# Expert coefficient operands placed at byte remainders 160 and 448 by 512 in place of 320

## The reference, cut to what matters

```
qry    = x @ w_query                          # 8 heads, two halves of 128
s1, s2 = scores of the halves against 128 keys each
best, pos = the 16 best of the 256 sums of the 16 best of each
gate   = softmax(best)                        # 16 experts per head and token
hid    = gelu(x . u_tab[expert])              # 16384 experts, width 2048
y      = sum over experts of gate * hid * v_tab[expert]
out    = rmsnorm(h + y)
```

## Time and profile before

| | |
|---|---|
| median of 3 runs | 3287.17 us (3283.33 to 3290.22) |
| the profiled execution, its own time | 3283.08 us |
| its span, first to last instruction | 3281.0 us |
| PE busy | 3215.3 us, 98% |
| weight loads busy (beside PE) | 2870.7 us, 87% |
| DVE, ACT, POOL busy | 2041.9, 1459.9, 495.7 us |
| mean DMA rate | 196 GB/s |
| granted TensorE clock, mean | 0.994 of full |

### The profile page before, as it was taken

One profiled execution on the slowest core, in us unless ns is written; L12 is line 12 of the kernel. 1 busy time (PEld: TensorE's weight loads), 2 busy tenths in 40 slices (PEclk: granted clock), 3 DMA queues, 4 the chain that ended last, 5 costly groups with the idle time before them and its releaser, 6 DMA issues.

```text
span 3281.0 us, 48331 instructions
## 1 busy us (share of the span) xinstructions
PE 3215.3 (98%) x20054; PEld 2870.7 (87%) x20054; DVE 2041.9 (62%) x1849; ACT 1459.9 (44%) x1268; POOL 495.7 (15%) x418
## 2 busy tenths in 40 slices
PE   7999999999999999999999999999999999999998
PEld 6788899999999878878879999999999888888886
DVE  4455665555555656765456788999984555555554
ACT  5554454433343463463335434555543433333333
POOL 0000000000000002225400000888850000000000
PEclk9999999999999999999999999999999999999999
DMA  6444465555555443342236566676776666566563
GB/s 257 143 165 158 163 221 193 192 192 191 192 192 191 154 167 120 124 157 100 83 136 231 187 219 219 225 243 239 257 250 238 250 256 234 226 243 254 226 247 117
DMA packets 131396, 644.18 MB, mean 196 GB/s; under 512 B 14640, under 2 KB 47664, under 8 KB 61872
## 3 DMA queue, kind: packets, MB, share of 16 engines
q1 hardware_dynamic: 96016, 624.18, 53.0%
q10 hardware_dynamic: 35232, 17.83, 1.8%
HBM read 606.31 MB, written 35.66 MB: 196 GB/s over the span
## 4 chain that ended last, share of the span: by engine, by line
PE 92%; DVE 3%; ACT 2%; DMA 1%; issue 1%; SPq 1%; DVEq 0%; ACTq 0%
PE pj L290 12%; PE pj L292 12%; PE pj L291 11%; PE pj L278 7%; PE pj L277 7%; PE pj L276 7%; PE pj L1640 3%; PE pj L1642 3%; PE pj L1641 3%; PE pj L821 3%; PE pj L823 3%; PE pj L822 3%; PE pm L278 2%; PE pt L278 2%; PE pt L277 2%; PE pm L277 2%
## 5 line engine op out<-in xcount | busy, mean ns | idle before, releaser
L258 ACT ACTIVATE hi<-raw 128x2048 fp32r<-128x2048 f32 x535 | 1025.2, 1917 | 1381.3 <-PE pj L292 640.7
L265 DVE TENSOR_TENSOR lo<-raw,hi 128x2048 fp32r<-128x2048 f32 x400 | 918.5, 2296 | 678.3 <-ACT hi L258 677.5
L290 PE MATMUL pj<-xh,hi 128*128 128x256 f32 x3328 | 919.9, 276 | 0.0
L291 PE MATMUL pj<-xl,hi 128*128 128x256 f32 x3328 | 918.8, 276 | 0.0
L292 PE MATMUL pj<-xh,lo 128*128 128x256 f32 x3328 | 918.8, 276 | 0.0
L291 PEld LDWEIGHTS pj<-xl,hi 128*128 128x128 f32 x3328 | 625.0, 188 | 0.6
L290 PEld LDWEIGHTS pj<-xh,hi 128*128 128x128 f32 x3328 | 624.8, 188 | 0.6
L292 PEld LDWEIGHTS pj<-xh,lo 128*128 128x128 f32 x3328 | 624.8, 188 | 0.0
L265 DVE TENSOR_TENSOR lo_in<-raw,hi 128x2048 fp32r<-128x2048 f32 x135 | 311.4, 2309 | 277.6 <-ACT hi L258 276.9
L2317 POOL TENSOR_SCALAR hotA<-cst,slotT 128x128 fp32r<-128x128 f32 x256 | 337.3, 1333 | 473.1 <-ACT slotT L2160 435.8
L1640 PE MATMUL pj<-hi,xh 128*128 128x512 f32 x576 | 235.7, 409 | 13.4 <-ACT proj L1709 7.3
(11 more groups left out here) (382 smaller groups left out, 4253.2 us busy)
## 6 DMA issues: line engine op xcount, KB each, us to landing
raw<-w_peer SPq DMA_DIRECT2D x256, 1024.0 KB, 6.4
raw<-w_mlp SPq DMA_DIRECT2D x128, 1024.0 KB, 4.8
raw<-w_in SPq DMA_DIRECT2D x104, 1024.0 KB, 4.8
raw<-w_out SPq DMA_DIRECT2D x32, 1024.0 KB, 4.8
raw<-w_q SPq DMA_DIRECT2D x16, 1024.0 KB, 4.9
act_scratch<-hidU SPq DMA_DIRECT2D x32, 512.0 KB, 3.3
gates_scratch<-stage ACTq DMA_DIRECT2D x8, 2048.0 KB, 17.1
hidV<-act_scratch SPq DMA_DIRECT2D x32, 512.0 KB, 3.5
```

Source lines behind the costliest of these rows:

```text
L258: nc.scalar.activation(hi[:, j, :], raw[:, j, :], ACT.Copy).then_inc(hi_ready, 1)
L265: nc.vector.tensor_tensor(low(q)[:, j, :], raw[:, j, :], hi[:, j, :].bitcast(F32), ALU.subtract).then_inc(lo_ready, 1)
L290: nc.tensor.matmul(o, hi[:, j, cols], xh[:, k0 + k, :], start=clears, stop=False, skip_group_check=True)
L291: nc.tensor.matmul(o, hi[:, j, cols], xl[:, k0 + k, :], start=False, stop=False, skip_group_check=True)
```

## The change

It gives each of the four coefficient operand tiles of the down stage a remainder. With `at_raw` at remainder 128, buffer 0 (even superblocks) is put at (128 + 32) mod 512 = 160 and buffer 1 (odd superblocks) at (128 + 320) mod 512 = 448.

```diff
         coefV = y("coefV", [P, 4, TT * P])
-        cV_h = [y(f"cV_h{i}", [P, 4, TT * P], F32R) for i in range(2)]
-        cV_l = [y(f"cV_l{i}", [P, 4, TT * P], F32R) for i in range(2)]
+        cV_h = [y(f"cV_h{i}", [P, 4, TT * P], F32R, rest=(at_raw + (32, 320)[i]) % 512) for i in range(2)]
+        cV_l = [y(f"cV_l{i}", [P, 4, TT * P], F32R, rest=(at_raw + (32, 320)[i]) % 512) for i in range(2)]
         last_sq = y("last_sq", [P, TT, D])
```

## The result

The changed kernel is slower: 3302.61 us (3298.41 to 3304.39, 5 runs) against 3287.17 us (3283.33 to 3290.22). The ratio is 1.0043, with a 95% interval of 1.0032 to 1.0054: small, but clear of noise. The time lies inside the range that was given (3266 to 3303), at its upper end, but the direction is not the one that was forecast. The profiled execution took 3298.41 us with a span of 3296.6, 15.6 us more than before.

What follows compares the result with a forecast made beforehand. PE's matmul stream alone was taken to bound the kernel. All terms were 0, so the profiled execution would stay at 3283.08 us; with the runs' median 4.1 above that, the forecast was 3287 us, range 3266 to 3303.

Steps and rivals of the forecast that it cites:

- step 1: Down stage, ACT's and DVE's writes of `cV_h` and `cV_l`: even if doubled, covered by slack; taken as 0.
- step 3: Down stage, weight loads: 188 ns beside a matmul step of 228.9, 41 ns free, so covered; taken as 0.
- the slower pattern: Same addresses, triples (three matmuls) of 700 against 686.7 ns: +6.8 us for even superblocks alone, +13.6 for both buffers.
- The rival with 0.25: Here the one forecasting a slower down stage: stream locks into the slower of two patterns, 3294 to 3304 us; chance 0.25.
- number 4: Down stage, matmul step: claimed not to depend on the distance between stationary and moving operand; 0 for both buffers.
- The slower rival: Down stage: matmul stream locks into the slower of two patterns, 13.3 ns a triple, 3294 to 3304 us; chance 0.25.
- The faster rival: Down stage: step's surplus over 215 ns is a conflict of PE's two reads, set by distance; 3244 to 3280 us; chance 0.25.
- the 13 ns of "waste": Down stage: each matmul step's excess over the skill formula's 215.8 ns for 512 columns, 40 us in the stage as estimate.

## Why the prediction was wrong

*What held.* PE's step alone decides this stage; nothing of the 13.6 us came by ACT, DVE, DMA or the clock. The writes (step 1) and the length of the weight load (step 3) kept their times, and both were covered. I had given the price of the slower pattern as 13.3 ns a triple, +13.6 us for both buffers; the stage grew by 13.6 us, and buffer 0 alone cost its half, 6.9 us of stage (buffer 1 alone 10.2, of which some 3 are the seven neighbours it drew along, 0.42 us each). The rival with 0.25 was the outcome. That the time fell inside the range is that rival's doing, as its price was the upper end; my own forecast was no change.

*The step that failed is number 4*, "I take 0 for the odd buffer" and "I take the value of the nearest rows, 0" for the even one. The step went from 228.9 to 233.3 ns in both, 13.6 us in place of 0. It rested on three rows, and each was too far away:

- L1452 shows no difference between distances 0 and 192, in 128-column plain fp32 products. The 512-column fp32r stream does differ there, 680 against 686.7 ns a triple. By 256, moreover, these two distances are its only fast places of eight: the rows compared the two that cost least.
- L1030 and L1031 at distance 0 are four matmuls behind an interruption. I read their 233 ns as "within 5 ns", when 4.4 ns was the whole effect in question.
- The up stage at -192 runs at 113.3 ns, and from that I drew that the odd buffer would be no slower. With the roles exchanged and twice the columns the map is another: -192, which is 64 by 256, is fast in the up stage and slow in the down stage.

The slower rival had the right price with a wrong condition, and the price was in part luck. It was taken from a pattern in which every triple takes 700 ns. In the changed kernel the triples go to and fro between about 698 and 702 ns and only their mean is 700, so it is the same pace but not the same pattern. The rival laid the cost on a start that is no multiple of 64 and on the phase at entry. Remainder 448, a multiple of 64, cost as much as 160, and the remainders 0, 192 and 256 as much or nearly so. The phase at entry does choose between two patterns at distance 192, but at the other six no superblock had a mean step below 232.2 ns, and at distance 0 none above 227.1. The faster rival was wrong for this change, yet a small part of what it hoped for exists at a distance that the change didn't take: 2.2 ns a matmul at distance 0. Its floor of 215 ns came from L635, which is no like row: 256 columns of plain float32 take 215 ns there, and 256 fp32r columns 113.5 in the up stage. No 512-column fp32r step below 226.7 ns was seen to hold.

The Trainium skill, page "TensorE: Matmul & The Clock Gate", section "Part 2: What happens when you issue a matmul", says that loading the next weights takes no read bandwidth from the running matmul. The load's duration keeps its median of 187 or 188 ns in the down stages of all kernels, in agreement; but the time from matmul to matmul depends on the two operands' distance, from 226.7 to 234.2 ns in the down stages and from 113.5 to 120.1 in the up stages, so in this kernel the two are not without effect on each other. The trace doesn't show the reads themselves. The formula that the prediction weighed, from the same page's section "Back-to-back issue gap", is given there for an isolated matmul, not for a stream with a load for each, so the 13 ns of "waste" don't follow from it.

*What stays open.* Why the period is 256 bytes, and what in PE or in its reads makes the patterns, no run tells. Distances that aren't multiples of 32 weren't tried. In the up stages only three distances were seen. Why one way of mixing two fast places (22.18 us) is slower than either is open too, and so is what in a passing stage sets the pattern of the next.

## What to carry to other kernels

When PE is busy all of the time, the relative placement of the stationary and the moving operand, here modulo 256 bytes, is worth a few tenths of a per cent to 2%, and is found only by trying: put a different remainder into each of two alternating buffers, and one profile gives two points of the map. Read the distance between starts of matmuls, not busy shares, and check every stage that shares a tile, since the best place of the down stages was the worst of three in the up stages. A change in one stage can also alter the steps of the next at unchanged addresses, so a gain in one is to be counted on the whole time.

## What the runs showed of the hardware that was not expected

- The step of uninterrupted 512-column fp32r matmuls depends on the operands' distance modulo 256 bytes: 226.7 to 227.1 ns at 0, 228.9 at 192 (at times 233.3), 232.2 to 234.2 at the other six multiples of 32.
- In the up stages, where loads follow one another without a gap, the order is another: 256-column matmuls take 113.5 ns at distance 64, 117.9 at 192, 120.1 at 0.
- At unchanged addresses a stream can hold either of two steps (113.5 or 117.8 ns, 228.9 or 233.3), and which one follows what ran before it. It can keep it over many chunks.
